# Down projection of the second block's feed-forward: six of eight output columns as column pairs in seven products instead of eight

## The reference

```python
def swiglu(x, w_gate, w_up, w_down):
    return (jax.nn.silu(x @ w_gate) * (x @ w_up)) @ w_down

h = h + 0.5 * swiglu(rmsnorm(h, norm_gains[l, 0]), ffn_w_gate[l, 0], ffn_w_up[l, 0], ffn_w_down[l, 0])
```

## Time and profile before

| what | value |
|---|---|
| three runs | 3684.9, 3685.34 (median), 3688.51 us |
| the profiled execution, its own time | 3684.85 us |
| its span, first to last instruction | 3683.1 us |
| PE busy | 3622.6 us, 98% of the span |
| DVE busy | 2537.3 us, 69% |
| ACT busy | 1632.3 us, 44% |
| POOL busy | 766.2 us, 21% |
| mean granted clock of TensorE | 0.998 |

### The profile page before, as it was taken

One profiled execution on the slowest core, in us unless ns is written; L12 is line 12 of the kernel. 1 busy time (PEld: TensorE's weight loads), 2 busy tenths in 40 slices (PEclk: granted clock), 3 DMA queues, 4 the chain that ended last, 5 costly groups with the idle time before them and its releaser, 6 DMA issues. The chain is left out here.

```text
span 3683.1 us, 64392 instructions
## 1 busy us (share of the span) xinstructions
PE 3622.6 (98%) x24518; PEld 3301.5 (90%) x24518; DVE 2537.3 (69%) x3684; ACT 1632.3 (44%) x2825; POOL 766.2 (21%) x661
## 2 busy tenths in 40 slices
PE   8999999999999999999999999999999999999999
PEld 5778888677888889999998999999999999899999
DVE  4677763566777386865668696779677565769667
ACT  3544332344433254544235554445445423746444
POOL 1111110012111022430003032334232001304322
PEclk9999999999999999999999999999999999999999
DMA  3122233212222323322110232332332212032333
GB/s 118 47 75 69 96 99 103 80 47 75 70 96 97 103 86 104 104 92 89 64 64 30 75 101 96 106 105 91 98 101 94 84 58 71 17 104 87 98 98 109
DMA packets 107207, 313.33 MB, mean 85 GB/s; under 512 B 30048, under 2 KB 32224, under 8 KB 106688
## 3 DMA queue, kind: packets, MB, share of 16 engines
q1 hardware_dynamic: 106384, 304.60, 25.5%
q0 software_dynamic: 560, 5.09, 0.4%
HBM read 307.48 MB, written 2.10 MB: 84 GB/s over the span
## 5 line engine op out<-in xcount | busy, mean ns | idle before, releaser
L716 ACT CAST w_hi<-stage 128x1024 fp32r<-128x1024 f32 x290 | 303.6, 1047 | 711.3 <-PE acc L2966 582.8
L2966 PE MATMUL acc<-x_hi,w_hi 128*128 128x264 f32 (+1 forms) x1984 | 543.1, 326 | 4.2 <-DVE w_lo L1580 3.5
L1580 DVE TENSOR_TENSOR w_lo<-stage,w_hi 128x1024 fp32r<-128x1024 f32 x290 | 397.7, 1371 | 206.6 <-ACT w_hi L716 200.7
L2966 PE MATMUL acc<-x_lo,w_hi 128*128 128x264 f32 (+1 forms) x1984 | 539.3, 324 | 0.0
L2966 PE MATMUL acc<-x_hi,w_lo 128*128 128x264 f32 (+1 forms) x1984 | 537.7, 324 | 0.0
L2177 DVE TENSOR_TENSOR w_lo<-stage,w_hi 128x512 fp32r<-128x512 f32 (+1 forms) x416 | 358.8, 865 | 146.4 <-ACT w_hi L1178 143.3
L1178 ACT CAST w_hi<-stage 128x512 fp32r<-128x512 f32 (+1 forms) x416 | 253.4, 610 | 318.2 <-PE acc L3572 271.6
L2966 PEld LDWEIGHTS acc<-x_hi,w_hi 128*128 128x128 f32 x1984 | 331.5, 188 | 45.6 <-issue 9.0
L3551 PE MATMUL misc<-t_hi,w_hi 128*128 128x264 f32 x1280 | 366.6, 286 | 0.0
L3551 PE MATMUL misc<-t_hi,w_lo 128*128 128x264 f32 x1280 | 363.3, 284 | 0.0
L3551 PE MATMUL misc<-t_lo,w_hi 128*128 128x264 f32 x1280 | 362.2, 283 | 0.0
(11 more groups left out here) (455 smaller groups left out, 8724.2 us busy)
## 6 DMA issues: line engine op xcount, KB each, us to landing
stage<-weights SPq DMA_DIRECT2D x568, 512.0 KB, 3.3
rotary_decay<-tables POOLq DMA_DIRECT2D x2, 2048.0 KB, 8.2
x<-x_in SPq DMA_DIRECT2D x4, 512.0 KB, 7.8
lse_rows<-lse_columns SPq DMA_DIRECT2D x128, 0.5 KB, 2.0
rotary_masks<-tables SPq DMA_DIRECT2D x2, 784.0 KB, 4.5
out<-x SPq DMA_DIRECT2D x8, 132.0 KB, 1.9
out<-x SPq DMA_DIRECT2D x8, 124.0 KB, 1.8
params<-params SPq DMA_DIRECT2D x2, 279.0 KB, 3.7
```

The costliest lines, as they stand in the source:

```text
L716: nc.scalar.copy(whi[p][:, :], stage[p][:, :]).then_inc(hi_ready, 1)
L1580: nc.vector.tensor_tensor(wlo[p][:, :], stage[p][:, :], whi[p][:, :].bitcast(F32), ALU.subtract).then_inc(lo_ready, 1)
L2966: ins = mm(ps[:, b, 0:tn], ww, act_[:, kt, t0:t0 + tn], start=start and n == 0 and q == 0, stop=stop and n == last and q == 2)
```

## The change

For the chunks of f0 to f7 and f8 to f15, output columns 2 to 7 are taken as three pairs (numbers 100 to 102 and 103 to 105), each by the same seven products as a gate/up pair: weight blocks of the two columns' strips, POOL's four sums of them, and token sums of the eight f tiles. Columns 0 and 1 of each chunk stay plain, and so does the whole down stage of the third chunk.

- PE: 252 matmuls (21 products) in place of 288 (12 blocks of 24) per such chunk.
- The f tiles are kept whole in float32 too (`whole`), and their four sums are made in place by DVE (`f_sum`, four of 128 x 1056), rounded by ACT (`f_sum_hi`), and the remainders made by DVE (`f_sum_lo`), per such chunk. f8 is copied once per feed-forward (`keep`).
- DVE per pair: seven `lo_block`, `c11`, `c22`, `c12`, and four additions to x of 128 x 264 (`onto_x`: x11, ug1, x22, x12; ug1 reads PSUM, the others the sum in `gate2`), in place of four `lo_block` and two `update`.
- ACT per pair: seven `hi_block`, `p1`, `u2`, `u3`, in place of four `hi_block`. POOL: four sums per pair, none before.
- SP: the same strips in the same order, but the strips of a pair are freed after POOL's sums too.
- Gate/up columns' banks, parts and counts are numbered along one chain over gate/up columns and pairs (`RANK2`, `before`, `behind`).

The diff, cut; its parts stand in the order SP, ACT, DVE, PE behind the lists.

```diff
+CHAIN2 = [n for j, (a, b, _, _) in enumerate(CHUNKS2) for n in list(range(a, b + 1)) + paired(j)]
+F_SUMS = ("S1", "S3", "S2", "A22")
...
+                    for n in paired(j):
+                        d = paired_column(n)
+                        read("A12", n)
+                        sp.wait_ge(pool_sum, s_count(q, n, 4))
+                        ring(STRIP2["d", d] + 4)
+                        read("A22", n)
+                        ring(STRIP2["d", d + 1] + 4)
...
+                        if n == b and j < 2:
+                            f_sum_hi(j, 0)
                         g2(n)
+                    if j < 2:
+                        f_sum_hi(j, 1)
                     f_hi_of_pair(b)
                     if j < 2:
-                        wait_blocks = 3 + 2 * (KT - 2)
-                        for _ in range(wait_blocks):
+                        f_sum_hi(j, 2)
+                        hi_block()
+                        f_sum_hi(j, 3)
+                        hi_block()
+                        hi_block()
+                        ev.up(2)
+                        p1(paired(j)[0])
+                        hi_block()
+                        for n in paired(j):
                             hi_block()
-                        ev.up(KT)
+                            u2(n)
+                            hi_block()
+                            hi_block()
+                            u3(n)
+                            hi_block()
+                            p1(behind(n))
+                            hi_block()
+                            hi_block()
+                            hi_block()
...
+                def onto_x(name, n):
+                    c = paired_column(n) % KT + (name in ("ug1", "x22"))
+                    xm = x[:, c, 0:HALF] if name in ("x11", "ug1") else x[:, c, HALF:TALL]
...
+                    nc.vector.scalar_tensor_tensor(xm, part, 0.5, xm, ALU.mult, ALU.add).then_inc(pair_sum, 1)
+                def keep(n):
+                    dve.wait_ge(pair_sum, sum_at(q, "ug2", KT))
+                    nc.vector.tensor_copy(FB[:, 0, :], US[:, :]).then_inc(pair_sum, 1)
+                def f_sum(j, a):
...
+                    left, right = ((1, 0), (2, 1), (2, 0), (3, 2))[a]
+                    nc.vector.tensor_tensor(whole_part(a), whole_part(left), whole_part(right), ALU.subtract).then_inc(xn_made, 1)
+                def f_sum_lo(a):
+                    dve.wait_ge(xh_ready, xhr.up())
+                    nc.vector.tensor_tensor(sum_lo(a), whole_part(a), sum_hi(a).bitcast(F32), ALU.subtract).then_inc(xl_ready, 1)
...
                         c22(n)
                         lo_block()
+                        if sums:
+                            f_sum(j, 0)
                         gate_first(n)
                         lo_block()
+                        if sums:
+                            f_sum(j, 1)
                         c12(n)
                         lo_block()
+                        if sums:
+                            f_sum(j, 2)
                     gate_second(b)
                     f_lo(b)
+                    if j < 2:
+                        f_sum(j, 3)
+                        lo_block()
+                        f_sum_lo(0)
+                        lo_block()
+                        update(KT * j)
+                        f_sum_lo(1)
+                        f_sum_lo(2)
+                        lo_block()
+                        update(KT * j + 1)
+                        lo_block()
+                        for n in paired(j):
+                            c11(n)
+                            lo_block()
+                            if n == paired(j)[0]:
+                                f_sum_lo(3)
+                            onto_x("x11", n)
+                            lo_block()
+                            lo_block()
+                            lo_block()
+                            c22(n)
+                            lo_block()
+                            onto_x("ug1", n)
+                            lo_block()
+                            onto_x("x22", n)
+                            c12(n)
+                            lo_block()
+                            onto_x("x12", n)
+                        continue
...
+                    if n >= PAIRED and (n - PAIRED) % 3 == 0 and name in F_SUMS:
+                        pe.wait_ge(xl_ready, xl0 + 2 * KT + 4 + 4 * ((n - PAIRED) // 3) + F_SUMS.index(name) + 1)
...
+                    for n in paired(j):
+                        if n == paired(j)[0]:
+                            xlr.up(4)
+                            p1(n)
+                        pair(n)
+                        p1(behind(n))
+                        pair_end(n)
-                    for c in range(2, KT - LATE if j == 2 and q % 2 else KT):
+                    for c in range(2, KT - LATE if q % 2 else KT) if j == 2 else ():
```

More of the change, by code:

```diff
@@ L80, with paired, paired_column, before @@
 CHUNKS2 = ((2, 8, 0, 8), (9, 16, 8, 16), (17, 21, 16, 22))
-NPAIR2 = FT - PLAIN2
+PAIRED = 100
+def paired(j):
+    return [PAIRED + 3 * j + m for m in range(3)] if j < 2 else []
+def paired_column(n):
+    return KT * ((n - PAIRED) // 3) + 2 + 2 * ((n - PAIRED) % 3)
+CHAIN2 = [n for j, (a, b, _, _) in enumerate(CHUNKS2) for n in list(range(a, b + 1)) + paired(j)]
+RANK2 = {n: i for i, n in enumerate(CHAIN2)}
+NPAIR2 = len(CHAIN2)
+def before(n, k=1):
+    return CHAIN2[RANK2[n] - k]
+def behind(n):
+    return CHAIN2[RANK2[n] + 1]
 ORDERS = ((0, 4, 1, 5, 2, 6, 3, 7), (0, 1, 2, 3, 4, 5, 6, 7))
@@ L101, in block_places @@
         names += [("Da", 8 * j + 1), ("Db", 8 * j), ("Db", 8 * j + 1)]
-        for c in range(2, KT):
+        for n in paired(j):
+            if n == paired(j)[0]:
+                names.append(("A11", n))
+            names += [("A12", n), ("S2", n), ("S1", n), ("S3", n), ("A11", behind(n)), ("A22", n), ("S4", n)]
+        for c in range(2, KT) if j == 2 else ():
             names += [("Da", 8 * j + c), ("Db", 8 * j + c)]
@@ L120, in pair_steps @@
                 sums.append(("ug2", n - 1))
+            elif j == 1:
+                sums.append(("kept", n))
             gates += [("g1", n), ("u2", n), ("u3", n)]
@@ L127, in pair_steps @@
         sums.append(("ug2", b))
+        for n in paired(j):
+            if n == paired(j)[0]:
+                gates.append(("p1", n))
+            gates += [("u2", n), ("u3", n), ("p1", behind(n))]
+            sums += [("c11", n), ("x11", n), ("c22", n), ("ug1", n), ("x22", n), ("c12", n), ("x12", n)]
     return {k: i + 1 for i, k in enumerate(sums)}, {k: i + 1 for i, k in enumerate(gates)}
@@ L702, in _ @@
             ffr, hb, yss = Tally(), Tally(), Tally()
-            strip = [0]
+            strip, turn = [0], [0]
             def chain(ins):
@@ L715, in split_hi @@
                 act.wait_ge(strip_done, free.up())
-                nc.scalar.copy(whi[p][:, :], stage[p][:, :]).then_inc(hi_ready, 1)
+                nc.scalar.copy(whi[(p + turn[0]) % 2][:, :], stage[p][:, :]).then_inc(hi_ready, 1)
             def wait_evacuated(k=1):
@@ L1563, in _ @@
             full, pout = Tally(), Tally(XR1)
-            strip, slot = [0], [0]
+            strip, slot, turn = [0], [0], [0]
             def link(ins, sem_, tally):
@@ L2922, in ffn2 @@
                     pool.wait_ge(x_ready, XR1)
-                s_sums(PLAIN2)
-                for n in range(PLAIN2 + 1, FT):
+                for n in CHAIN2:
                     s_sums(n)
@@ L3506, in ffn2 @@
             def ffn2(q):
-                base, p0, f0, xl0 = NB2 * q, strip[0] % 2, ffr.up(FT) - FT, xlr.now()
+                base, w0, f0, xl0 = NB2 * q, (strip[0] + turn[0]) % 2, ffr.up(FT) - FT, xlr.now()
                 def first_two():
@@ L3891, in merge_tiles @@
             def merge_tiles(k, bank, tiles):
-                p = (strip[0] + k) % 2
+                p = (strip[0] + k + turn[0]) % 2
                 for t in tiles:
```

227 lines of the change are left out of this document (149 added, 78 removed).

## The result

The changed kernel takes 3703.69 us (median of five runs, 3700.9 to 3709.41), the kernel before 3685.34 in the same number of runs. The ratio is 1.0049, with a 95% interval of 1.0034 to 1.0064: slower, by 18 us. The forecast was 3700. All its lines stand further down in the code, and in its trace the first passage starts 1.83 us earlier than in that of the kernel before.

What follows compares the result with a forecast made beforehand. The prediction took PE, busy 98% of the span, as the bound. Per changed chunk, -4.4 saved + 5.4 stall + 0.85 after it = +1.9 us, times eight +15 on 3684.85: 3700 us, range 3664 to 3722.

Steps and rivals of the forecast that it cites:

- What is saved: 36 matmuls of 264 columns fewer per changed chunk, 4.4 us each chunk, 35.1 us over eight, all on PE's path.
- The passage: From column 8's c22 through the first pair: DVE's list with POOL's turns makes S4 start 5.4 us late.
- The walk: DVE's list followed from c22 of column 8: S2 starts at 1443.8, c22 of the first pair is done at 1452.7.
- rival B: At the first pair, POOL's turns fall into DVE's waits or run under other instructions: stall 0.6 us, 3658 us; chance 0.14.
- A second wait before A22 or S4: Sign of being right: in each of eight passages PE stands again there, after 3 to 4 us before S2.
- The pair stage: Per pair DVE needs 10.0 us and PE 10.23, so PE is the bound, by 0.2 us.
- the 10.5 that the prediction named as a sign of being wrong: Pairs running at over 10.5 us each would show the forecast wrong; 10.2 to 10.3 with no wait was expected.
- Rival D: The pairs are bound by DVE too: +0.5 us in three pairs, +1.5 a chunk, 3712 us; chance 0.08.
- After it: Next gate/up stage starts with little DVE lead, and with `keep` loses 0.85 us per chunk, ends 0.2 and 1.7.
- Rival E: PE's two waits bring a fall of the granted clock to 0.50 in each passage, 1.0 us: +8, 3708 us; chance 0.06.
- The sum: Per changed chunk -4.4 + 5.4 + 0.85 = +1.9 us, times eight +15, making 3700 us.

## Why the prediction was right, and some of its prices wrong

- **What is saved.** 36 matmuls at 0.1218 us per chunk, as said. Nothing to correct.
- **The passage.** S4 of the first pair was forecast 5.4 us late. It is 5.4 to 5.5 late in five of the eight passages, and 6.2 to 6.8 in the other three. The walk met S2's start within 0.1 us, and the end of c22 of the first pair too (1452.7 less 1.83 is 1450.87; it ends at 1450.94). POOL's turns came in the number and at the price that were taken. There are three up to ug2 (f_sum 0, the w_lo behind it and f_sum 1: 1.10 + 0.77 + 1.09), and three more behind S2 (two w_lo and f_sum_lo 3: 0.66 + 0.75 + 1.09, against 2.5). The run without these turns shows that they decide the sign: rival B's stretch of 0.6 us is what it found before S2 (0.67), and its other side came true there, 23 us faster. That POOL's first sum hides in DVE's wait was so in seven of eight passages; in the eighth it cost 0.7 us.
- **One sign was missing.** A second wait before A22 or S4 was said to be seen in each passage. In the profiled execution it is nowhere over 0.3 us, because PE is still slow or has just been. Where the clock is held up, or does not fall, it is there, 1.34 and 1.36 us.
- **The pair stage.** x12 took 1.52 us and x11, x22 0.42, the values taken. PE has no wait of note in pairs two and three. Still, pair two takes 10.38 to 10.55 us, 10.53 to 10.55 in six of the eight passages. That is 0.3 us over PE's pace, which the sum had at nothing, and just above the 10.5 that the prediction named as a sign of being wrong. Pair three takes 10.22 to 10.24 in four passages and 10.33 to 10.54 in the others. Rival D's 0.5 us in each of three pairs did not come, but a fifth of it did. DVE is busy for 10.23 of the 10.55 us; what makes the steps longer, no run here isolates.
- **After it.** 0.85 us was forecast. Behind the passage the steps sum to 1.1 us on average over the eight stretches, against 0.6 before. So this term is 0.5, a little over half of what was taken. This and the 0.3 to 0.4 us more up to the end of pair two cancel, and that is luck. Da of column 1 to A11 of the next chunk takes 45.2 to 45.4 us in five passages, as forecast, and 46.2 to 46.8 in three.
- **The clock.** Rival E's event came in all eight passages of the profiled execution, though it had a chance of 0.06. Its price of 1.0 us was read from a part of a fall (2.6 of its 3.4 us); the whole one takes 12 of 28 matmuls, 1.5 us of work. But this price was not paid either, because the fall lies where PE has a wait of 1.5 us ahead of it in any case. Only the two longer falls cost, about 2.5 us together. That part of the rival should have been checked against the walk, which had the second wait in it.
- **The sum.** +1.9 us a chunk was forecast. In the second trace of the changed kernel it is (879.4 - 864.4) / 8 = 1.9; in the first, with the longer falls, 2.3. The median of 3703.69 is 3.7 above the forecast.

The Trainium skill (SBUF — State Buffer, "Who interferes with whom") says that a VectorE instruction with two SBUF inputs and one of GpSimd that reads SBUF exclude each other. The trace agrees, for a form that the kernel before did not show beside POOL: x12 takes 1.52 us there, and x11 of the same size 0.42.

## What to carry to other kernels

A product scheme that takes matmuls away pays with vector work, and here much of that work comes at the scheme's start, not spread over it: set the vector engine's list against the matmuls that cover it at that place, with each turn in which it has to wait for another engine, before counting the saving. If the list is too long, changing its order can move the wait and keep its sum, as here; more plain work ahead of the scheme, at the price of a smaller saving, can give more than the full scheme. Look for a second wait behind the first before pricing what is taken away, or what a slow clock costs.

## What was not expected of the hardware

- A wait of 3.15 us of PE, with 12 matmuls before it and full work around, was followed by a fall of the granted clock to its lower level in all eight passages of one execution, six times for 3.4 us (16 matmuls in place of 28, 0.51 and 0.53 in the windows shown) and twice for 6.8. The same wait was followed by it in five of the eight of another execution of the same kernel. With 28 idle matmuls in the wait it was in none. Why three passages with the same wait were spared, no run here shows.
- A shorter wait can do it too. With the low parts in another order the longest wait of a passage is 1.93 to 1.96 us, and the clock fell behind it in four of the eight, for the first time at 1445.76 (18 matmuls in 3.41 us at 0.50).
- Such a fall can be free. It cost nothing where the engine had to wait a little later, and 1.2 to 1.4 us where it lasted 6.8 us.
